# A fused two-block transformer step on one core: the long-convolution filters are made at the start from one packed load, and three transfers change their place

## The reference, cut to what matters

```python
def hyena_filters(L, w1, b1, w2, b2, w3):
    ...
    z = jnp.concatenate([t, jnp.cos(ang), jnp.sin(ang)], axis=-1)      # (256, 33), constant
    h = jnp.sin(z @ f32(w1) + f32(b1))                                 # 64 wide
    h = jnp.sin(h @ f32(w2) + f32(b2))
    h = (h @ f32(w3)).reshape(L, HYENA_ORDER, 2, D_HYENA)              # 2 orders, 2 sides, 512
    return h * jnp.exp(-t * deltas)[:, None, None, :]

def bidir_long_conv(u, h, skip):
    k = jnp.concatenate([h[:, 0], jnp.zeros((1, C), h.dtype), h[:0:-1, 1]], axis=0)
    U = jnp.fft.rfft(u, n=2 * L, axis=1)
    Kf = jnp.fft.rfft(k, n=2 * L, axis=0)
    y = jnp.fft.irfft(U * Kf[None], n=2 * L, axis=1)[:, :L]
    return y + u * skip

def first_block(...):
    ada_x = jnp.split(s_lat @ w_ada[l] + b_ada[l], 6, axis=-1)         # shifts and scales
    hc = modulate(rmsnorm(ctx, norm_mix_g[l]), ada_c[0], ada_c[1])     # context
    hx = modulate(rmsnorm(x, norm_mix_g[l]), ada_x[0], ada_x[1])       # tokens
    ...                                                                # h @ w_in: keys, values, queries, ...
```

## Time and profile before

| what | value |
|---|---|
| median of 3 runs | 2405.12 us (2401.39 to 2405.33) |
| the profiled execution: its own time | 2403.52 us |
| its span, first to last instruction | 2401.7 us |
| busy share of the span: PE, DVE, ACT, POOL | 85%, 33%, 30%, 42% |
| chain that ended last: PE, DMA | 58%, 34% |
| moved by DMA | 680.04 MB |

### The profile page before, as it was taken

One profiled execution on the slowest core, in us unless ns is written; L12 is line 12 of the kernel. 1 busy time (PEld: TensorE's weight loads), 2 busy tenths in 40 slices (PEclk: granted clock), 3 DMA queues, 4 the chain that ended last, 5 costly groups with the idle time before them and its releaser, 6 DMA issues.

```text
span 2401.7 us, 31563 instructions
## 1 busy us (share of the span) xinstructions
PE 2041.8 (85%) x13298; PEld 1421.7 (59%) x13298; DVE 784.1 (33%) x1502; ACT 718.3 (30%) x854; POOL 1002.8 (42%) x327
## 2 busy tenths in 40 slices
PE   8999997666666655666669999999999999999998
PEld 5788882111211111111128887888887887888887
DVE  4575652111111111111112345433312253534332
ACT  2245420000000000000004545544543454644452
POOL 1356630000000000000007764887887774877886
PEclk9999999787878888788889999999999999999999
DMA  8584489999999999999998543566656653565653
GB/s 327 156 281 160 169 353 407 427 427 428 428 429 428 428 429 428 428 428 428 428 423 293 167 158 117 173 193 205 207 191 208 213 162 118 176 182 185 218 187 132
DMA packets 245600, 680.04 MB, mean 283 GB/s; under 512 B 8638, under 2 KB 173520, under 8 KB 218931
## 3 DMA queue, kind: packets, MB, share of 16 engines
q1 hardware_dynamic: 241600, 671.88, 74.0%
q10 hardware_dynamic: 3075, 4.65, 0.7%
q0 software_dynamic: 816, 1.94, 0.3%
HBM read 673.85 MB, written 4.59 MB: 282 GB/s over the span
## 4 chain that ended last, share of the span: by engine, by line
PE 58%; DMA 34%; DVE 4%; POOL 1%; issue 1%; ACT 1%; POOLq 0%; ACTq 0%; SPq 0%; DVEq 0%
PE bank L2124 57%; DMA ring_sb<-w_exp 33%; PE bank L2127 2%; POOL ring_parts L851 1%; DMA ring_sb<-w_in 1%; DVE bank L1286 1%; DVE sm_sb L2045 0%; ACT ring_parts L1113 0%; DVE arena_sb L1283 0%; DVE x_sb L1286 0%; DVE sm_sb L2048 0%; DVE bank L1283 0%; DVE sm_sb L1870 0%; DMA fb_sb<-hy_f_b 0%; DMA ring_sb<-w_ffn_down 0%
## 5 line engine op out<-in xcount | busy, mean ns | idle before, releaser
L851 POOL TENSOR_TENSOR ring_parts<-ring_sb,ring_parts 128x2048 fp32r<-128x2048 f32 (+2 forms) x185 | 843.8, 4574 | 1205.2 <-ACT ring_parts L1113 1204.6
L2124 PE MATMUL bank<-arena_sb 128*32 128x512 f32 (+10 forms) x2862 | 373.3, 543 | 133.2 <-DMA arena_sb<-w_exp 119.4
L2124 PE MATMUL bank<-arena_parts,ring_parts 128*128 128x256 f32 (+1 forms) x2480 | 481.2, 329 | 2.2 <-issue 1.3
L2124 PE MATMUL bank<-hT_parts,ring_parts 128*128 128x256 f32 (+1 forms) x2208 | 462.7, 326 | 2.6 <-issue 2.3
L2124 PE MATMUL bank<-ring_sb,arena_sb 128*32 128x512 f32 (+1 forms) x2240 | 272.1, 629 | 193.9 <-DMA ring_sb<-w_exp 193.7
L1113 ACT CAST ring_parts<-ring_sb 128x2048 fp32r<-128x2048 f32 x186 | 351.1, 1887 | 208.8 <-DMA ring_sb<-w_in 92.0
L2124 PEld LDWEIGHTS bank<-arena_parts,ring_parts 128*128 128x128 f32 x2480 | 385.1, 190 | 46.8 <-issue 2.1
L1283 DVE TENSOR_TENSOR arena_sb<-bank,arena_sb 128x512 f32<-128x512 f32 (+4 forms) x240 | 139.1, 601 | 781.8 <-PE bank L2124 687.9
L2124 PEld LDWEIGHTS bank<-hT_parts,ring_parts 128*128 128x128 f32 x2208 | 357.2, 191 | 40.0 <-issue 5.1
L2124 PEld LDWEIGHTS bank<-arena_sb 128*32 128x32 f32 (+5 forms) x2862 | 151.6, 143 | 326.9 <-DMA arena_sb<-w_exp 173.2
L2124 PEld LDWEIGHTS bank<-ring_sb,arena_sb 128*32 128x32 f32 x2240 | 73.3, 127 | 378.7 <-DMA ring_sb<-w_exp 284.4
(11 more groups left out here) (277 smaller groups left out, 1329.0 us busy)
## 6 DMA issues: line engine op xcount, KB each, us to landing
ring_sb<-w_exp SPq DMA_DIRECT2D x96, 2048.0 KB, 36.1
arena_sb<-w_exp SPq DMA_DIRECT2D x93, 2048.0 KB, 36.1
ring_sb<-w_in SPq DMA_DIRECT2D x92, 1024.0 KB, 5.3
ring_sb<-w_ada SPq DMA_DIRECT2D x24, 1024.0 KB, 8.7
ring_sb<-w_ffn_gate SPq DMA_DIRECT2D x22, 1024.0 KB, 5.3
ring_sb<-w_ffn_up SPq DMA_DIRECT2D x22, 1024.0 KB, 5.3
ring_sb<-w_ffn_down SPq DMA_DIRECT2D x22, 1024.0 KB, 4.9
ring_sb<-w_in SPq DMA_DIRECT2D x42, 512.0 KB, 5.4
```

The lines of the kernel that those rows point to most:

```text
L851: g.tensor_tensor(low, half(n)[0], high.bitcast(F32), ALU.subtract).then_inc(s["lo_ready"], 1)
L2124: return M.matmul(o, l, r, start=first, stop=last)
```

## The change

- **Packed filter inputs.** One load of 128 by 450 values (`pack_f`) replaces six small loads and `dftw`. Its constant row of ones and the biases as a row of the weights replace the bias additions in `sine_arg`. The second sine layer has its weights twice side by side, so that its result fills 128 partitions; ACT applies the sine twice, the second time with the sign of the upper half turned.
- **Sum and difference at once.** `w3` is packed with the two sides stacked on 128 partitions, so a filter product gives the sum (or, from the sign-turned copy, the difference). The stage `filt_sum` on DVE goes; POOL adds the skip to row 0 of both.
- **Order.** All eight filter products come before the slabs; `pack_ac` comes after `hx`; the eight spectra (`spec0`, `spec5`, `spec6`) stand between the slabs, behind `adacol0`, and no longer behind `kc`.
- **Transfers.** `w3` is loaded ahead of slot 0, `dft` by SP behind slot 1; POOL's biases and table inputs are issued behind the first sine; ACT issues the write of `rel_table` and the load of `half_dft` behind the high part of the tokens, where both stood behind the keys.
- **ACT's order.** The casts of the two value slots come before the context keys are emptied.

```diff
 def plan_units():
...
+    u.add("sin2", 1)
+    u.add("filt0", 4)
+    u.add("filt1", 4)
+    u.add("ada0.0", 1, "A")
+    u.add("hx", 4, "A")
     u.add("pack_ac", 1)
-    u.add("sin2", 1)
-    u.add("filt0", 3)
-    u.add("ada0.0", 1, "A")
-    u.add("filt3", 1)
     u.add("reltab", 1)
-    u.add("hx", 4, "A")
-    u.add("filt4", 1)
+    u.add("spec0", 5, "AV")
     u.add("ada0.1", 1)
-    u.add("filt5", 1)
+    u.add("spec5", 1)
     u.add("adacol0", 1)
-    u.add("filt6", 2)
     u.add("unused", 5)
+    u.add("spec6", 2, "AV")
     u.add("kx", 2, "A")
     u.add("hc", 4, "AV")
     u.add("kc", 2, "A")
-    u.add("filtK", 8, "AV")
     u.add("ada1.0", 1, "A")
...
 @block.gpsimd
...
+            pool.wait_ge(s["sin1_ready"], 1)
             for dst, src in pack_ac_loads:
...
+            for o in range(2):
+                pool.wait_ge(s["freed_dve"], U.count[U.at("filt0", 2 * o + 1)])
+                g.tensor_tensor(filt[0:1, 0, o], filt[0:1, 0, o], skipb[:, o * 512:(o + 1) * 512].unsqueeze(1).broadcast_to([1, 2, 512]),
+                                ALU.add).then_inc(s["skip_added"], 1)
...
 @block.scalar
...
+            act.dma_start(pack_f, a["pack_f"]).then_inc(s["filter_landed"], 16)
...
-            A.activation(sv[0:64, 3], sv[0:64, 2], ACT.Sin).then_inc(s["sin2_ready"], 1)
+            A.activation(sv[:, 3], sv[:, 2], ACT.Sin).then_inc(s["sin2_ready"], 1)
+            A.activation(sv[:, 1], sv[:, 2], ACT.Sin, scale=cst[:, 3:4]).then_inc(s["sin2_ready"], 1)
...
+            for i in (0, 2, 4):
+                spectrum("spec0", i, i)
...
+            spectrum("spec6", 0, 6)
             act.wait_ge(s["x_mod_act"], KD - BY_DVE)
             act.wait_ge(s["x_mod_dve"], BY_DVE)
             A.copy(hx_pair[0], modulated).then_inc(s["x_high"], 1)
+            act.wait_ge(s["rel_ready"], 1)
+            act.dma_start(rel_table, relbuf.unsqueeze(1).broadcast_to([AH, P, 384])).then_inc(s["rel_saved"], 16)
+            act.wait_ge(s["unit_done"], U.at("spec6", 1) + 1)
+            act.dma_start(arena[:, 24616:25640], k["half_dft"]).then_inc(s["half_dft_landed"], 16)
             act.wait_ge(s["ctx_var"], 1)
             A.activation(sm[:, 10:12], sm[:, 6:8], ACT.Sqrt).then_inc(s["ctx_sqrt"], 1)
...
-            raw("kc", 2, 16, 2)
-            act.wait_ge(s["rel_ready"], 1)
-            act.dma_start(rel_table, relbuf.unsqueeze(1).broadcast_to([AH, P, 384])).then_inc(s["rel_saved"], 16)
             high_part(S_V)
             high_part(S_V + 1)
-            act.wait_ge(s["tables_landed"], 16 * len(table_loads))
-            for i in range(0, 8, 2):
-                b = take("filtK", i)
...
+            raw("kc", 2, 16, 2)
             ada_row(1, 0)
-            act.wait_ge(s["unit_done"], U.at("filtK", 7) + 1)
-            act.dma_start(arena[:, 24616:25640], k["half_dft"]).then_inc(s["half_dft_landed"], 16)
...
 @block.vector
...
-            difference = region(29096, 512)
-            for t in range(2):
-                for o in range(2):
-                    link(tt(difference, filt[:, t, o, 0], filt[:, t, o, 1], ALU.subtract))
...
 @block.tensor
...
+            keep_clock(bank[U.at("sin1") % 8], 6)
+            pe.wait_ge(s["w3_landed"], 16)
+            filter_rows(0)
+            filter_rows(1)
             b = open_unit("ada0.0")
             ada_slab(b, 0)
...
             close(ada_slab(b, 1))
-            filter_rows("filt3", 3, 1)
+            pe.wait_ge(s["x_norm"], 1)
+            turn("hx", xn)
...
+            pe.wait_ge(s["tables_landed"], 16)
+            pe.wait_ge(s["skip_added"], 2)
+            wait_emptied(pe, "filt1")
+            spectrum("spec0", 0, 0)
             b = open_unit("ada0.1")
             ada_slab(b, 2)
-            filter_rows("filt4", 4, 1)
-            keep_clock(open_unit("filt5"), 12)
+            for i in range(1, 5):
+                spectrum("spec0", i, i)
             close(ada_slab(b, 3))
-            filter_rows("filt5", 5, 1)
+            spectrum("spec5", 0, 5)
...
-            filter_rows("filt6", 6, 2, unused=5)
+            for i in range(2):
+                spectrum("spec6", i, 6 + i)
...
-            pe.wait_ge(s["filt_sum"], 1)
-            pe.wait_ge(s["tables_landed"], 16 * len(table_loads))
-            for i in range(8):
-                o, f, q = i // 4, (i // 2) % 2, i % 2
-                b = open_unit("filtK", i)
...
             ada_product(1, 0)
```

More of the change, by code:

```diff
@@ L877, in root @@
                 A.activation(dst, src, ACT.Sqrt).then_inc(s["sqrt_ready"], 1)
[L880 to L883, removed]
+            act.dma_start(pack_f, a["pack_f"]).then_inc(s["filter_landed"], 16)
+            act.dma_start(skipb, a["hy_skip"].rearrange("a o c -> a (o c)")).then_inc(s["skip_landed"], 16)
             act.wait_ge(s["cst_set"], 2)
@@ L906, in _, with spectrum @@
                 give(A.copy(modulated[:, 2 * i:2 * i + 2].rearrange("p k t -> p (k t)"), take("hx", i)[:]))
-            for dst, src in table_loads:
-                act.dma_start(dst, src).then_inc(s["tables_landed"], 16)
+            def spectrum(name, j, i):
+                o, f, q = i // 4, (i // 2) % 2, i % 2
+                give(A.activation(filtK[:, o, q, f], take(name, j)[:], ACT.Identity, scale=dftw[:, f:f + 1]))
+            for i in (0, 2, 4):
+                spectrum("spec0", i, i)
             cast = [0]
@@ L1330, in mean_square, with filter_products, spectrum @@
                     link(V.bn_aggr(sm[:, 16 + 2 * (t0 + t):18 + 2 * (t0 + t)], bn[:, t0 + t].rearrange("p h c -> p (h c)")))
[L1331 to L1336, removed]
+            def filter_products(t):
+                for j in range(4):
+                    give(tt(filt[:, t, j // 2, j % 2], take(f"filt{t}", j)[:], win[:, t]))
+            def spectrum(name, j, i):
+                o, f, q = i // 4, (i // 2) % 2, i % 2
+                give(V.tensor_scalar(filtK[:, o, q, f], take(name, j)[:], dftw[:, f:f + 1], None, ALU.mult))
             def ada_row(batch, i):
@@ L1361, in _ @@
             ins.then_inc(s["x_norm"], 1)
-            filter_products("filt0", 1, 2, 1)
-            filter_products("filt3", 3, 1)
+            filter_products(1)
+            b = take("pack_ac")
+            V.tensor_copy(colA[:, 0:108], b[:, 0:108])
+            give(V.tensor_copy(colC[:].rearrange("p (l c) -> p l c", l=2)[:, :, 0:66],
+                               b[:, P:3 * P].rearrange("p (l c) -> p l c", l=2)[:, :, 0:66]))
             b = take("reltab")
@@ L1403, in _ @@
             dve.sem_inc(s["m_ready"], 1)
-            filter_products("filt6", 6, 2, unused=5)
+            spectrum("spec6", 1, 7)
             def modulate(name, dst3, g0, src, sh0=0):
@@ L1467, in _ @@
             conv(3, kcT[:, 2:4], D_MLC + 6, 8, 1, U.at("kc", 1))
-            for i in range(1, 8, 2):
-                b = take("filtK", i)
-                o, f, q = i // 4, (i // 2) % 2, i % 2
-                give(V.tensor_scalar(filtK[:, o, q, f], b[:], dftw[:, f:f + 1], None, ALU.mult))
             dve.wait_ge(s["vaug_ones"], 1)
@@ L2210, in ada_turn, with filter_rows, spectrum @@
                     close(ins)
-            def filter_rows(name, i0, n, unused=0):
-                for j in range(n):
-                    t, c = divmod(i0 + j, 4)
-                    b = open_unit(name, j)
-                    ins = mm(b[:], sv[0:64, 3, t * P:(t + 1) * P], w3[0:64, 512 * c:512 * c + 512])
-                    ins.then_inc(s["unit_done"], 1 if j < n - 1 else 1 + unused)
-                for i in range(unused):
-                    open_unit("unused", i)
+            def filter_rows(t):
+                for j in range(4):
+                    o, side = divmod(j, 2)
+                    b = open_unit(f"filt{t}", j)
+                    if t == 0:
+                        pe.wait_ge(s["sin2_ready"], side + 1)
+                    close(mm(b[:], sv[:, 3 - 2 * side, t * P:(t + 1) * P], w3[:, o]))
+            def spectrum(name, j, i):
+                o, f, q = i // 4, (i // 2) % 2, i % 2
+                b = open_unit(name, j)
+                for t in range(2):
+                    ins = mm(b[:], dft[:, q, t, f * P:(f + 1) * P], filt[:, t, o, q], t == 0, t == 1)
+                close(ins)
             def keep_clock(b, n):
@@ L2279, in _ @@
                 ins = tr(b[:, c * P:(c + 1) * P], adarows[0][:, 0, c * P:(c + 1) * P])
-            close(ins)
-            filter_rows("filt6", 6, 2, unused=5)
+            ins.then_inc(s["unit_done"], 6)
+            for i in range(5):
+                open_unit("unused", i)
+            for i in range(2):
+                spectrum("spec6", i, 6 + i)
             def spread(name, dg):
@@ L2324, in _ @@
             gemm_slot_T(S_KC, "kc", 0, modulated, "hc")
-            pe.wait_ge(s["filt_sum"], 1)
-            pe.wait_ge(s["tables_landed"], 16 * len(table_loads))
-            for i in range(8):
-                o, f, q = i // 4, (i // 2) % 2, i % 2
-                b = open_unit("filtK", i)
-                for t in range(2):
```

(4 more changed lines are left out.)

105 lines of the change are left out of this document (48 added, 57 removed).

## The result

The changed kernel takes 2409.82 us (median of 20 runs, 2406.91 to 2412.06), the kernel before 2404.32 (20 runs, 2400.32 to 2408.56): ratio 1.0023, 95% interval 1.0017 to 1.0030. It is slower by 5.5 us; predicted were 2410. The profiled execution took 2412.06, its span is 2410.3 us where it was 2401.7, so by the two traces it is 8.6.

The account below looks back on a forecast made before the run. TensorE was taken to bound the kernel up to the expert layer; 9.1 us gained would be eaten by a stop of some 12 us: 4.4 + 1.5 = 5.9 us later, so 2410 us, range 2396 to 2416.

Parts of the forecast that it names:

- What bounds the kernel: TensorE sets the pace up to the expert layer; a shift of ada1.0 moves the end one for one.
- The filling, 9.1 us earlier: Spectra moved into TensorE's partly idle time ahead of the keys: keys at 46.2, ada1.0 at 76.1 in place of 85.25.
- the sum: TensorE's stage ahead of the keys rebuilt from its rows: keys at 46.2, ada1.0 at 76.1 without a held issue.
- POOL's additions: Skip additions beside the normalising of x, ahead of the keys: cost between 0 and some 2.5 us, taken 0 to 1.
- The held issue: On ACT, half_dft's issue waits until rel_table's write has mostly drained, 22.7 us after the write's issue, delaying the context's root.
- U: Time at which ACT is free for the context's root: 68.7 as held before, taken 70.5, bounds 64.8 and 73.4.
- From U on: Root, normalised context, low part, then context keys at U + 5.3 = 75.8; ada1.0 13.9 later at 89.7, 4.4 us later.
- The slow restart: TensorE slower after standing still from 60.1 to 72.4, ahead of the context keys: 1.5 us, between 0 and 2.5.
- The median: Whole kernel: 2409.4 against the profiled execution, 2411.0 against the median of three runs; forecast 2410.
- The issue isn't held: Rival on ACT's queue: ACT is free before the keys are done, the 9.1 us remain, 2394.4; chance 0.20.
- The stop is longer: Rival ahead of the context keys: U at 76 or later, 12 us or more, from 2415.5; chance 0.06.
- the filling doesn't work: Rival: no idle time ahead of the keys, which start at 55; with no hold 2403.5; chance 0.04.

Follow-up runs that it names:

- both edits: Changed kernel with POOL's skip additions waiting for normalised x and half_dft issued behind ada_row(1, 0); 2394.42 us, 0.9967 to the kernel before.

## Why the prediction was right

*What bounds the kernel.* Right. Over the kernels run here `ada1.0` moved from 76.42 to 92.84, 16.4 us, and the rest of the span from there stayed between 2312.6 and 2318.6 us, except with the whole write late, where TensorE waited for `w_ada` (2325.9).

*The filling, 9.1 us earlier.* Right where the additions and the hold are out of the way: with both edits `ada1.0` stands at 76.42 where the sum has 76.1, and 9.4 us are gained. Two errors nearly cancel there: `hx` starts 0.8 earlier than in the sum, and the first spectrum waits 1.65 for the moved additions. In the changed kernel itself the keys came at 51.3, not 46.2. The term that was mis-sized is POOL's additions: I took 0 to 1 with a bound of 2.5, `hx` came 2.4 later than in the sum, and behind that wait it was 2.7 more to the keys, for a lower clock that the sum did not have at all (24.5 from `hx` to the keys, 21.2 at the full clock, 21.8 in the sum). The row for such a delay was read the earlier trace rows, and the bound from it held; the value taken was the wrong end of it.

*The held issue.* The mechanism was right, and so was its size: 22.2 us from the write's issue to the end of the hold, 22.7 before. My correction of U upwards, for more loads ahead of the write, was too large (24.5): the write was issued 5.0 later, when SP's loads were nearly through (25 packets of them from there to the end of the hold), and its first packet came after 2.2 us, where it was about 5 before. With the write at 46.58, nearly where the sum has it, the hold was 23.0, so a correction of 0.3 was due there, not 1.8. U came at 73.2 (taken 70.5, bounds 64.8 and 73.4): 5.0 for the later write, 2.3 back for the shorter hold. That the second hid almost half of the first was luck. "Until the write has mostly drained" was wrong in its wording: it is until its last 620 to 750 packets.

*From U on.* The context keys at U + 5.4 (5.3 predicted). The slow restart was there, `hc` took 3.68 in place of 1.9, and the trace says what it is: the lower level of the clock (columns as in the earlier trace rows).

```profile
75.15:78.60 3.45, 3.45 (x16) 3.41 (x17) 3.14 (x3) 1.27 (x3) 0.00 (x0) 0.50 0.57 145
```

Most of it passes while the context keys would have waited for the scaled context anyway; 0.3 remained of my 1.5. So `ada1.0` came at 92.84, 1.6 later than the sum with its restart, 91.2: 5.0 - 2.3 + 0.1 - 1.2. TensorE stood for 9.9, not 12, since the keys were late too.

*The median.* 8.6 us by the traces, 5.5 by the medians: the profiled execution of the changed kernel lay 2.2 above its median, that of before 0.8 below. In it the clock from 205 to 225 us was 0.83, where before had 0.91, and that accounts for 1.7 of the 8.6 (a piece of the chain there took 46.12 us against 44.45); the same piece took 42.97 to 46.15 over these kernels, whatever was edited, and 46.12 in both traces of the changed kernel. That the median lies 0.2 from the forecast is luck in part: terms that were off by 5.0, 2.3 and 1.2 left only 1.6, and single executions of the changed kernel lie up to 3 us from its median.

*Rivals.* *The issue isn't held* had the right price, 2394.4, and the wrong condition: both edits together gave 2394.42. What the Trainium skill, DMA: Bandwidth & Descriptors, section Issuing engines are not separate DMA queues, says of an issue's own time, that it is usually small beside the transfer, holds for 0.36 and 0.54 us here and not for 21.27: the runs decide, and what decides in them is the backlog of the issuing engine's own queue. *The stop is longer* and *the filling doesn't work* are out.

## What to carry to other kernels

A transfer that is issued on an engine which also computes is an instruction in that engine's program: before it is put behind a large write on the same queue, look at what stands behind it on the engine, and who waits for that. Count what is in front in packets, since a backlog of 576 cost nothing here and one of 2,304 some 21 us; an issue moved behind the urgent work or onto POOL's queue took the whole stop away. Ask, too, what the moved transfer will meet: the late write cost TensorE 5.3 us elsewhere. And when a stage is packed tighter, look at the short waits that are left in it: here one of 2.8 us cost up to 3.3 more through the clock, in some executions and not in others.

## What the runs showed of the hardware

- An issue on ScalarE's queue, behind a write of 2,304 packets and 0.95 us after the write's issue, was held 20.3 to 22.1 us; behind 1,152 packets 9.4, behind 576 not at all; in the traces where it was held, 619 to 746 packets of the write were left when it came free. On POOL's queue, 0.76 us after the write's issue, it took 0.54; on SP's, with 1,258 packets of the write to go on ScalarE's, another load took 0.37.
- Two additions on one partition on POOL, 2.4 and 2.8 us, held back DVE's two normalisings, 0.7 us each by itself: 1.8 and 2.8 beside them, and each ended some 0.55 us behind the end of an addition. DVE's products with the window, one operand of which lies in PSUM, took 2.48 for four beside them and without them. The Trainium skill, SBUF — State Buffer, section SBUF: two separate sides, has DVE and GpSimd lock a pair of ports for a whole instruction, for DVE's faster modes or two operands in SBUF; these rows agree with it.
- The same wait of TensorE, 2.6 to 2.8 us at the same place, was followed by a clock of 0.62 to 1.00 over nine microseconds, differently in different executions of programs that were alike up to there. With no wait there, or with the wait filled, it was 1.00 (three traces). The 9.9 us of standing ahead of `hc` were followed by a clock of 0.50 from 75.15 to 78.6.
